# Retention's projections ahead of its heads, 15 of 16 block pairs as seven products of 384 columns

## The chip, the cores and the metric

The kernel runs on one core of a Trainium2 chip, in fp32 data. The metric is the device time of one execution in microseconds. The profile is one execution recorded by the hardware profiler; its times count from the start of the span.

## The reference, cut to the changed part

The whole program is two transformer blocks. The first layer of the second block mixes its tokens by retention: 4 heads, 512 latent and 256 context tokens (768 columns in all, the context being the last 256), width 1024, 256 query and key columns and 512 value and gate columns a head. With the additions on both sides cut away:

```python
def retention_mixer(a_ctx, a_lat, w_in, decay_param, w_out, want_ctx):
    log_gamma = -jnp.exp(decay_param.astype(jnp.float32))
    def project(a, rope):
        q, k, v, g = jnp.split(a @ w_in, [hk, 2 * hk, 2 * hk + hv], axis=-1)
        ...
        if rope is not None:
            q, k = apply_rope(q, *rope), apply_rope(k, *rope)
        k = k * RET_DK ** -0.5
        ...
    ctx_terms, g_ctx = project(a_ctx, None)
    lat_terms, g_lat = project(a_lat, axial_rope(L, RET_DK))
    o_ctx, o_lat = bidirectional_scan(ctx_terms, lat_terms)
    def readout(o, g):
        y = rms_norm_2(o).transpose(0, 2, 1, 3).reshape(B, n, hv).astype(g.dtype)
        return (jax.nn.silu(g) * y) @ w_out
```

A weight of the scan depends only on the distance of two tokens and on the head, so the kernel computes it as scores, times a table of decays (one for each head, both directions summed), times values. The result of all heads, through w_out, is added to the tokens, and a layer norm of the context and of the latent tokens follows.

## The kernel before

Every fp32 product is made of three products of parts: an operand is split into a rounded part (hi) and the rest (lo), and TensorE runs hi by hi, hi by lo, lo by hi (L2113, L2114, L2115). Weights come through a ring of three raw slots of 512 KB on SyncE's DMA queue (`t_raw`); ScalarE casts the hi part (`t_whi`, L2435), VectorE (L2810) or GpSimd (L3494) subtracts to get the lo part (`t_wlo`).

`schedule()` writes the items of the program in order, and `Plan` then lays the instructions of each engine out in one fixed order by estimated costs. So each engine runs a static queue: an instruction that waits for a semaphore holds back all that stand behind it on its engine, its DMA issues too.

Retention, in `retention()`, goes head by head. `v_rows(h)` makes the values with tokens as rows, `decays(h)` builds the head's table from a table of distances (VectorE L3315 to L3327, ScalarE L2679 to L2682, two exponentials), `queries_keys(h)` makes four blocks of 128 query and key columns (a block of 512 latent and one of 256 context columns each, so 96 matmuls for two blocks), turns them by rope and splits them, and `attend(h)` makes scores, decayed scores and values for 6 tiles of keys. `gates(h)` then makes four blocks of gate columns; between them VectorE computes the root mean square (a reciprocal at L3399), the normed values (L3405), the gated values (L3409) and their lo parts (L3414), for each block of 512 and 256 columns. Last comes the output product (`ret_o`), which reads those parts, with the next head's `v_rows` and `decays` ahead of it. In the last head there is no next head, the context's columns go first, and the layer norm of the context tokens runs on VectorE while the latent columns' products go on.

Elsewhere the kernel has a form of product that the change takes up: in the three feed-forward parts (`seven_products`), two blocks of weights by two groups of 384 tokens and two halves of the depth are multiplied with seven products in place of eight. A block matrix product with quarters A11 to A22 of the weights and B11 to B22 of the tokens is made of seven products: P1 = A11 B11, P2 = A12 B21, P3 = S4 B22, P4 = A22 T4, P5 = S1 T1, P6 = S2 T2, P7 = S3 T3, where S1 to S4 are sums of weight quarters (VectorE, `wadd`) and T1 to T4 sums of token quarters (`token_sums`, `last_sums`). P1, P6 and P7 accumulate one on another in one PSUM bank, and P5 and P3 in another, so the bank is copied out (`snap`, ScalarE) between them, and VectorE adds the copies to what comes after (`seven_add`). A product is 12 matmuls of 384 columns.

## Time and profile before

| what | value |
|---|---|
| time, median of 3 runs | 2790.18 us (2788.88 to 2790.49) |
| the profiled execution, its span | 2789.8 us |
| TensorE busy | 2760.5 us, 99% of the span |
| VectorE busy | 1891.0 us, 68% |
| ScalarE busy | 1236.5 us, 44% |
| GpSimd busy | 405.2 us, 15% |
| retention, from its first value matmul to its last output matmul | 916.25 to 1572.25 us |

The profiled execution's span lies inside the range of the three times, so what is around the span is under a microsecond. A busy share is taken over the whole span; a matmul's own time overlaps that of the one behind it, so the rate of TensorE is read from start to start, or from a stretch and its count of matmuls, and not from mean times. A slice of the page is a fortieth of the span, 69.7 us: retention covers slices 14 to 23.

### The profile page before, as it was taken

How to read it: one execution, taken by the hardware profiler on the slowest of the kernel's cores; microseconds unless marked ns; L12 is line 12 of the kernel's file. 1: busy time of each engine (PE TensorE's matmuls, PEld its weight loads, DVE VectorE, ACT ScalarE, POOL GpSimd, SP SyncE). 2: the span in 40 equal slices, each digit the busy share in tenths (PEclk: the TensorE clock that was granted, in tenths of full speed). 3: DMA queues.
4: the chain of work that ended last, by engine and by line, in shares of the span. 5: the costliest groups of instructions: out<-in, count | busy, mean ns of one | idle time of the engine just before them, and what ended most of it. 6: DMA issues, size and time to landing. Idle time of an engine off the chain costs nothing.

```text
span 2789.8 us, 42554 instructions
## 1 busy us (share of the span) xinstructions
PE 2760.5 (99%) x16554; PEld 2456.6 (88%) x16554; DVE 1891.0 (68%) x3427; ACT 1236.5 (44%) x2249; POOL 405.2 (15%) x222
## 2 busy tenths in 40 slices
PE   8999999999999999999999999999999999999998
PEld 8888896988888888888888999999997787989898
DVE  7788788868896653444435896566685636777686
ACT  5332358642233552332314654344355546545354
POOL 2233300023323011011011000000001323000000
PEclk9999999999999999999999999999999999999999
DMA  6565512236554211111011112222223121222322
GB/s 206 186 187 190 165 64 83 84 102 222 189 188 137 77 53 61 38 61 61 31 61 53 40 57 79 63 67 72 72 76 102 50 76 52 76 84 91 106 92 84
DMA packets 86025, 267.91 MB, mean 96 GB/s; under 512 B 9153, under 2 KB 18753, under 8 KB 85569
## 3 DMA queue, kind: packets, MB, share of 16 engines
q1 hardware_dynamic: 85824, 265.20, 29.6%
q8 instruction: 131, 2.15, 0.3%
q14 instruction: 70, 0.57, 0.1%
HBM read 261.49 MB, written 2.10 MB: 94 GB/s over the span
## 4 chain that ended last, share of the span: by engine, by line
PE 94%; DVE 3%; ACT 1%; issue 1%; DMA 1%; SPq 0%; DVEq 0%; ACTq 0%
PE ps L2113 30%; PE ps L2114 29%; PE ps L2115 29%; PE ps L2392 1%; PE ps L2376 1%; PE ps L2365 1%; DMA t_x<-in_x 0%; DVE t_wlo L2810 0%; PE ps L2257 0%; PE ps L2249 0%; PE ps L2308 0%; PE ps L2265 0%; PE ps L2298 0%; DVE t_m L3128 0%; DVE t_m L2927 0%
## 5 line engine op out<-in xcount | busy, mean ns | idle before, releaser
L2113 PE MATMUL ps<-t_h,t_whi 128*128 128x512 f32 (+2 forms) x2152 | 726.7, 338 | 7.7 <-DVE t_tmp L2840 3.2
L2114 PE MATMUL ps<-t_h,t_wlo 128*128 128x512 f32 (+2 forms) x2152 | 721.2, 335 | 0.0
L2115 PE MATMUL ps<-t_h,t_whi 128*128 128x512 f32 (+2 forms) x2152 | 721.1, 335 | 0.0
L2435 ACT CAST t_whi<-t_raw 128x1024 fp32r<-128x1024 f32 (+3 forms) x449 | 367.8, 828 | 570.5 <-PE ps L2115 372.6
L2113 PEld LDWEIGHTS ps<-t_h,t_whi 128*128 128x128 f32 x2152 | 407.9, 190 | 51.0 <-issue 10.4
L2114 PEld LDWEIGHTS ps<-t_h,t_wlo 128*128 128x128 f32 x2152 | 408.0, 190 | 36.5 <-issue 1.2
L2115 PEld LDWEIGHTS ps<-t_h,t_whi 128*128 128x128 f32 x2152 | 407.9, 190 | 35.6
L2113 PE MATMUL ps<-t_hid,t_whi 128*128 128x256 f32 (+2 forms) x1320 | 428.2, 324 | 1.8 <-DVE t_hid L3107 1.7
L2114 PE MATMUL ps<-t_hid,t_wlo 128*128 128x256 f32 (+2 forms) x1320 | 425.7, 322 | 0.0
L2115 PE MATMUL ps<-t_hid,t_whi 128*128 128x256 f32 (+2 forms) x1320 | 425.1, 322 | 0.0
L2810 DVE TENSOR_TENSOR t_wlo<-t_raw,t_whi 128x512 fp32r<-128x512 f32 (+3 forms) x360 | 321.7, 903 | 111.8 <-ACT t_whi L2435 108.7
L3494 POOL TENSOR_TENSOR t_wlo<-t_raw,t_whi 128x1024 fp32r<-128x1024 f32 (+1 forms) x89 | 219.4, 2465 | 902.1 <-ACT t_whi L2435 902.1
L3059 DVE CUSTOM_DVE_ANT_0 t_m<-t_raw,t_m 128x1024 f32<-128x1024 f32 x192 | 297.8, 1588 | 44.7 <-DMA t_raw<-in_ada 36.8
L2113 PEld LDWEIGHTS ps<-t_hid,t_whi 128*128 128x128 f32 x1320 | 251.1, 190 | 22.1 <-DVE t_hid L3107 2.2
L2115 PEld LDWEIGHTS ps<-t_hid,t_whi 128*128 128x128 f32 x1320 | 251.0, 190 | 18.6
L2114 PEld LDWEIGHTS ps<-t_hid,t_wlo 128*128 128x128 f32 x1320 | 251.2, 190 | 18.2
L3494 POOL TENSOR_TENSOR t_xw<-t_raw,t_xw 128x1024 fp32r<-128x1024 f32 (+1 forms) x8 | 21.4, 2670 | 724.4 <-DVE t_x L3128 517.1
L2113 PE MATMUL ps<-t_mw,t_whi 128*128 128x256 f32 (+1 forms) x394 | 121.4, 308 | 0.0
L2114 PE MATMUL ps<-t_mw,t_wlo 128*128 128x256 f32 (+1 forms) x394 | 121.3, 308 | 0.0
L2115 PE MATMUL ps<-t_mw,t_whi 128*128 128x256 f32 (+1 forms) x394 | 121.3, 308 | 0.0
L3128 DVE SCALAR_TENSOR_TENSOR t_m<-ps,t_mod,t_m 128x512 f32<-128x512 f32 (+1 forms) x79 | 51.2, 648 | 80.4 <-PE ps L2115 80.3
L2113 PE MATMUL ps<-t_wlo,t_h 128*128 128x512 f32 x264 | 104.0, 394 | 0.0
(357 smaller groups left out, 4836.5 us busy)
## 6 DMA issues: line engine op xcount, KB each, us to landing
t_raw<-in_gu SPq DMA_DIRECT2D x174, 512.0 KB, 3.4
t_raw<-in_ada SPq DMA_DIRECT2D x96, 512.0 KB, 3.8
t_raw<-in_dn SPq DMA_DIRECT2D x52, 512.0 KB, 4.2
t_raw<-in_dn SPq DMA_DIRECT2D x24, 384.0 KB, 3.4
t_raw<-in_ret_v SPq DMA_DIRECT2D x16, 512.0 KB, 3.3
t_raw<-in_ret_qk SPq DMA_DIRECT2D x16, 512.0 KB, 3.3
t_raw<-in_ret_g SPq DMA_DIRECT2D x16, 512.0 KB, 3.4
t_raw<-in_ret_o SPq DMA_DIRECT2D x16, 512.0 KB, 3.8
```

What stands on the lines that cost most here:

```text
L2113: e.matmul(out, whi, xlo, start=first, stop=False, skip_group_check=shared)
L2114: e.matmul(out, wlo, xhi, start=False, stop=False, skip_group_check=shared)
L2115: return e.matmul(out, whi, xhi, start=False, stop=last, skip_group_check=shared)
L2365: done = e.matmul(m.PS[:, hd, :].rearrange("p (a t) -> p a t", a=2), m.na_q(qpart, it.c, it.b * P, P)[pp], m.na_keys(kpart, it.c, BAND0[it ...
L2376: done = e.transpose(m.PS[:, 2 + hd, kt * P:(kt + 1) * P], s[:, kt * P:(kt + 1) * P], m.ident)
L2392: done = e.matmul(m.PS[hd * 64:hd * 64 + 64, 4 + hd, it.b * P:(it.b + 1) * P], m.at(v, 64), m.na_t(it.to[hd])[:, kt // 2, kt % 2 * P:(kt % ...
L2435: e.copy(m.block(0, it.slot, n), m.raw(it)).then_inc(*S["hi"].of(j))
L2810: e.tensor_tensor(m.block(1, it.slot, n), m.raw(it), m.block(0, it.slot, n), ALU.subtract).then_inc(*S["lo_dve"].of(j))
L3059: e.tensor_tensor_reduce(m.at(ADA_OUT + who * 1024, 1024), m.RAW[:, it.raw % NR, :], m.cond(who), 1.0, 0.0, ALU.mult, ALU.add, m.mod(it.la ...
L3128: e.scalar_tensor_tensor(out=out, in0=ps, scalar=m.mod(it.layer, it.who, it.gm, it.j), in1=old, op0=ALU.mult, op1=ALU.add).then_inc(*S["dr ...
L3494: e.tensor_tensor(m.block(1, it.slot, n), m.raw(it), m.block(0, it.slot, n), ALU.subtract).then_inc(*S["lo_pool"].of(j))
```

## The change

In the new kernel all projections of retention come first, and the heads follow.

1. The first head's values are made as before, but aside (in the tile `HID`), and stored to device memory (`s_v`, two halves of 1.5 MB).
2. The token sums T1 to T4 for 384 columns are made for retention too. The four heads' decay tables are built one behind another in one place (`RTAB`), and each is stored (`s_dec`, 768 KB); the next one may overwrite the place only when the store is done (`late`, the semaphore `d_ds`).
3. One pair of gate blocks (head 1, the first) is made in the plain way with stores to `s_g`. The other 15 pairs, in the order of heads 1, 2, 3, 0 and in each head two query/key pairs and then its gate pairs, are made by `seven_pair`, with rope on halves of 384 columns and stores to `s_qk` and `s_g`. Head 0's queries and keys stay in place.
4. Then, for each head, `attend(h)`, `v_rows(h + 1)` and `ret_o`, with the tables, the queries and keys and the gates loaded back on SyncE's queue, between the loads of weights. The gates' products no longer stand between the values and the output product. Normed and gated values are written to a place of their own (`ret_yr`).

The stores are issued on ScalarE's queue. The diff, cut to its core:

```diff
+        def decays(h, after):
+            put("ret_decay", h=h, after=after, slot=[e for k in range(4) for e in slots.get(("b", k), [])])
             free([("b", k) for k in range(4)], ("ret_gs", h))
-            ov["p"][0] = ov["p"][0] + [("ret_act", ("ll", h))]
-            ov["p"][1] = ov["p"][1] + [("ret_act", ("ll", h))]
+            put("dec_store", h=h)
+            return [("d_ds", h)]
...
+        def plain_gates(h, i):
+            def post(g, c):
+                off, after, keys_ = tmp("a", g.n)
+                half = 2 + g.t0 // 512
+                put("g_plain", h=h, c=c, half=half, g=g.id, bank=g.bank, t0=g.t0, n=g.n, off=off, after=after)
+                gate_store(h, c, half, g.t0, g.n, off, keys_, f"d_gp{off // 256}")
+            columns([(("ret_g", h * 4 + c), (SLOT,), DC, ("h", 4), [(0, "drain_act", lambda g, c=c: post(g, c))]) for c in (2 * i, 2 * i + 1)], SEG2)
...
+        def seven_pair(what, h, i):
+            key, n = ("ret", what, h, i), 384
+            ops = pair(*((("ret_qk", i * 8 + h * 2 + k) if what == "qk" else ("ret_g", h * 4 + 2 * i + k)) for k in range(2)))
+            banks = {"P1": bank(), "P2": bank(), "P5": bank()}
+            banks.update(P6=banks["P1"], P7=banks["P1"], P4=banks["P1"], P3=banks["P5"])
+            ids = {}
+
+            def product(name, q, x, before):
+                j = ops[q]
+                ready(j)
+                g = put("seven", w=j, slot=where[j], lo=low[j], name=name, f="ret", ver=4, x=x, n=n, bank=banks[name],
+                        first=name in ("P1", "P2", "P5"), before=before)
+                ids[name] = g.id
+                tick(4 * (n + 32) / 800)
+                over(j, "ps", g.id)
+
+            def snap(name):
+                off, after, keys_ = wide(n, "a")
+                put("snap", key=(*key, name), g=ids[name], bank=banks[name], n=n, off=off, after=after)
+                return off, keys_
...
+            product("P1", "A11", "B11", seat(banks["P1"], "drain_dve" if what == "qk" else "drain_act", (*key, "C21")))
+            s1, keys1 = snap("P1")
+            product("P5", "S1", "T1", seat(banks["P5"], "drain_dve", (*key, "C12")))
+            s5, keys5 = snap("P5")
+            product("P6", "S2", "T2", [("snap", (*key, "P1"))])
+            s2, keys2 = snap("P6")
+            offs, at = {(0, 0): s1, (0, 1): s2, (1, 1): s5}, (0, 1, 2, 3)
+            product("P3", "S4", "B22", [("snap", (*key, "P5"))])
+            add("C12", "P6", s2, "P3")
+            if what == "g":
+                gate("C12", 0, 1, s2, keys2)
+            product("P7", "S3", "T3", [("snap", (*key, "P6"))])
+            add("C22", "P5", s5, "P7")
+            if what == "g":
+                gate("C22", 1, 1, s5, keys5)
```

(The rest of a pair is P2 with C11 and P4 with the last quarter; for queries and keys the rope operations stand in place of the gates' silu.) The order of the whole:

```diff
+        ov["v"] = state["hid_free"]
         v_rows(0)
-        pro = state["misc_free"]
-        put("ret_setup", after=pro)
-        ov.update(oc=pro, p=[pro, pro, pro], st=pro, sg={0: pro, 512: pro})
-        decays(0)
+        put("v_store")
+        pro = state["misc_free"] + [("ps", ("root", "nf2", s)) for s in range(2)] + [("ada", (1, 47, who)) for who in range(2)]
+        put("ret_setup", after=pro + state["hid_free"])
+        token_sums("ret", 4, 384, pro)
+        last_sums("ret", 4, 384, pro)
+        late = pro
         for h in range(n_head):
-            queries_keys(h)
+            late = decays(h, late)
+        put("rope_load", after=[("ret_act", ("ll", n_head - 1))])
+        sides[:] = [late] * 4
+        plain_gates(1, 0)
+        wide_slots(384)
+        ov["qk"] = [[("d_vs0", 0)], [("d_vs0", 0)]]
+        state["quad"] = [("gate_pool", ("f2", "rs", s)) for s in range(2)]
+        for h in (1, 2, 3, 0):
+            for w in range(2):
+                seven_pair("qk", h, w)
+            for w in range(h == 1, 2):
+                last = seven_pair("g", h, w)
+        back_to_slots(384)
+        last_h = [("ps", last["P4"])]
+        rope_done = sides[0] + sides[1] + sides[2] + sides[3]
+        put("dec_load", h=0, after=rope_done + [("d_ds", n_head - 1)])
+        put("v_load", after=[("ps", last["P6"])])
+        put("g_load", h=0, after=last_h + stores[0])
+        ov.update(oc=last_h, p=[rope_done, rope_done, last_h], v=[])
...
```

On ScalarE, at the start of the projections, the old kernel has the following behind the last rows of values (`t_mw<-ps`): casts of weights, the exponentials of head 0's table, and then the scaling of the tokens by alpha (L2523).

```order
L2576 CAST t_mw<-ps 128x512 [waits ps]
L2435 CAST t_whi<-t_raw 128x1024 [waits ps,d_ring0]
L2576 CAST t_mw<-ps 128x512
L2679 ACTIVATE t_m<-t_m 128x896 [waits ret_dve]
L2681 ACTIVATE t_m<-t_m,t_tmp 128x640
L2682 ACTIVATE t_tmp<-t_m,t_tmp 128x640
L2695 CAST t_hid<-t_tmp 128x512 [waits qk]
L2523 ACTIVATE t_x<-t_x 128x256 [waits h_hi]
L2523 ACTIVATE t_x<-t_x 128x256
```

In the new kernel, behind the casts of the last token sums (L2604) come the decays' first exponential with a table load, the stores of the values, and the same scaling of the tokens (L2661, three in a row with a wait, eight times: the first rows of it here).

```order
L2604 CAST t_mw<-t_m 128x384 [waits t_full] x4
L2810 ACT_TABLE_LOAD
L2810 ACTIVATE t_tmp<-t_par 128x8
L2832 DMA s_v<-t_hid 128x3072 [waits drain_act,drain_dve]
L2832 DMA s_v<-t_hid 128x3072
L2661 ACTIVATE t_x<-t_x 128x256 [waits h_hi]
L2661 ACTIVATE t_x<-t_x 128x256 x2
```

Behind these and four casts stand the silu of the plain gate pair (L2851), its stores (L2864) and the copies of P1 and P5 out of PSUM (L2578).

```order
L2851 ACTIVATE t_tmp<-ps 128x512 [waits h_lo]
L2851 ACTIVATE t_tmp<-ps 128x256 [waits h_lo]
L2864 DMA s_g<-t_tmp 128x512 [waits drain_act]
L2864 DMA s_g<-t_tmp 128x256 [waits drain_act]
L2573 CAST t_whi<-t_raw 128x512 [waits ps,wadd]
L2573 CAST t_whi<-t_tmp 128x512 [waits ps,wadd]
L2851 ACTIVATE t_tmp<-ps 128x512 [waits d_gp0]
L2851 ACTIVATE t_tmp<-ps 128x256 [waits d_gp2]
L2864 DMA s_g<-t_tmp 128x512 [waits drain_act]
L2864 DMA s_g<-t_tmp 128x256 [waits drain_act]
L2578 COPY t_tmp<-ps 128x384 [waits d_gp0]
L2578 COPY t_tmp<-ps 128x384 [waits d_gp2]
```

So the silus (`t_tmp<-ps`), before spread under the gates of each head, now stand behind the token scaling, and of the second blocks' silus and the copies each waits for a store (`d_gp0`, `d_gp2`).

A little further on ScalarE stand the last two of the four tables, and then the copy of P6 out of PSUM.

```order
L2817 ACTIVATE t_m<-t_m 128x896 [waits d_ds,ret_dve]
L2819 ACTIVATE t_m<-t_lru,t_tmp 128x640
L2820 ACTIVATE t_tmp<-t_lru,t_tmp 128x640
L2825 DMA s_dec<-t_m 128x1536 [waits ret_gs,ret_ll]
L2817 ACTIVATE t_m<-t_m 128x896 [waits d_ds,ret_dve]
L2819 ACTIVATE t_m<-t_lru,t_tmp 128x640
L2820 ACTIVATE t_tmp<-t_lru,t_tmp 128x640
L2578 COPY t_tmp<-ps 128x384 [waits ret_gs,h_lo]
L2825 DMA s_dec<-t_m 128x1536 [waits ret_ll]
```

Before, one table was built in each head, with no store, as these rows of VectorE show:

```order
L3315 TENSOR_SCALAR t_m<-t_m,t_tmp 128x896 [waits x_sum,ret_dve,d_misc]
L3318 TENSOR_SCALAR t_tmp<-t_m,t_tmp 128x896 [waits hid_lo]
L3321 TENSOR_TENSOR t_m<-t_m,t_tmp 128x896 [waits ret_dve]
L3324 TENSOR_TENSOR t_m<-t_m,t_con 128x128 [waits ret_act]
L3327 TENSOR_TENSOR t_m<-t_m,t_tmp 128x640 [waits ret_act]
L3340 TENSOR_TENSOR t_tmp<-ps,t_m 128x512 [waits ret_gs,ps]
```

Now VectorE's row of the last table waits for the store of the one ahead (`d_ds`), and its first sum of the first pair (L3003) stands behind all four.

```order
L3491 TENSOR_TENSOR t_m<-t_m,t_tmp 128x640 [waits ret_act]
L3479 TENSOR_SCALAR t_m<-t_lru,t_tmp 128x896 [waits d_ds]
L3482 TENSOR_SCALAR t_tmp<-t_lru,t_tmp 128x896 [waits ret_gs]
L3485 TENSOR_TENSOR t_m<-t_m,t_tmp 128x896 [waits ret_dve]
L3488 TENSOR_TENSOR t_m<-t_m,t_con 128x128 [waits ret_act]
L3491 TENSOR_TENSOR t_m<-t_m,t_tmp 128x640 [waits ret_act]
L3003 TENSOR_TENSOR t_tmp<-t_tmp,ps 128x384 [waits snap,ps]
L3003 TENSOR_TENSOR t_tmp<-t_tmp,ps 128x384 [waits ps]
```

What moved: the copy of P6 (`snap`, L2578) stands behind all four tables on ScalarE, and so does the first `seven_add` on VectorE.

On SyncE's queue, around the end of the last pair, the loads for the first head stand behind the loads of the next weights:

```order
L2148 DMA t_raw<-in_ret_v 128x1024 [waits lo_dve,hi] x3
L2148 DMA t_raw<-in_ret_v 128x1024 [waits lo_pool,hi]
L2148 DMA t_raw<-in_ret_o 128x2x512 [waits lo_dve,hi]
L2148 DMA t_raw<-in_ret_o 128x2x512 [waits lo_pool,hi]
L2195 DMA t_m<-s_dec 128x1536 [waits rq_lo,d_ds,rq]
L2202 DMA t_mw<-s_v 128x1024 [waits d_vs0,ps]
L2202 DMA t_mw<-s_v 128x1024
L2205 DMA t_mw<-s_v 128x2048 x2
L2214 DMA t_m<-s_g 128x4x512 [waits d_gs2,d_gs5,d_gs1,d_gs0,d_gs3,d_gs4,ps]
L2215 DMA t_m<-s_g 128x4x256
```

Before, this head's table and gates were not loaded at all.

In the last head, VectorE had, before, reciprocal, norm, gate and lo part under the gates' products:

```order
L3399 RECIPROCAL t_tmp<-t_tmp 128x512 [waits drain_act]
L3405 TENSOR_TENSOR t_m<-t_m,t_tmp 128x512 [waits ret_dve]
L3409 TENSOR_TENSOR t_m<-t_m 128x512 [waits drain_act,ret_n]
L3405 TENSOR_TENSOR t_m<-t_m,t_tmp 128x256
L3409 TENSOR_TENSOR t_m<-t_m 128x256 [waits drain_act,ret_n]
L3405 TENSOR_TENSOR t_m<-t_m,t_tmp 128x512
L3414 TENSOR_TENSOR t_hid<-t_m,t_hid 128x512 [waits ret_act]
L3414 TENSOR_TENSOR t_hid<-t_m,t_hid 128x256 [waits ret_act]
L3409 TENSOR_TENSOR t_m<-t_m 128x512 [waits drain_act,ret_n]
L3405 TENSOR_TENSOR t_m<-t_m,t_tmp 128x256
L3414 TENSOR_TENSOR t_hid<-t_m,t_hid 128x512 [waits ret_act]
```

Now these rows come behind one another with the context's output product and layer norm between them (`t_x<-ps` is the output product's sum, L3092 and L3173 belong to the norm):

```order
L3575 RECIPROCAL t_tmp<-t_tmp 128x512 [waits drain_act]
L3293 SCALAR_TENSOR_TENSOR t_x<-ps,t_mod,t_x 128x256 [waits ps] x3
L3092 TENSOR_TENSOR t_m<-t_m,t_x 128x256 [waits drain_dve,acc] x3
L3098 TENSOR_TENSOR t_m<-t_m 128x256 [waits acc]
L3581 TENSOR_TENSOR t_m<-t_m,t_tmp 128x512 [waits ret_dve]
L3173 TENSOR_TENSOR t_x<-t_x,ps 128x256 [waits ps]
L3173 TENSOR_TENSOR t_x<-t_x,ps 128x256 x4
L3092 TENSOR_TENSOR t_m<-t_m,t_tmp 128x256 [waits sq,acc_act] x2
L3092 TENSOR_TENSOR t_m<-t_m,t_tmp 128x256 [waits sq,acc]
L3173 TENSOR_TENSOR t_x<-t_x,ps 128x256 x3
L3092 TENSOR_TENSOR t_m<-t_m,t_tmp 128x256 [waits sq,acc] x3
L3098 TENSOR_TENSOR t_m<-t_m 128x256 [waits acc]
```

and, some rows on, to the four lo parts (L3590) for which the latent output product waits:

```order
L3158 TENSOR_SCALAR t_tmp<-t_con,t_st 128x128
L3581 TENSOR_TENSOR t_m<-t_m,t_tmp 128x512
L3207 SCALAR_TENSOR_TENSOR t_x<-t_x,t_par,ps 128x256 [waits ps,x_mid]
L3207 SCALAR_TENSOR_TENSOR t_x<-t_x,t_par,ps 128x256 [waits x_mid] x7
L3213 TENSOR_TENSOR t_h<-t_tmp,t_h 128x256 [waits h_hi,h_full]
L3585 TENSOR_TENSOR t_m<-t_m 128x512 [waits ret_n]
L3581 TENSOR_TENSOR t_m<-t_m,t_tmp 128x512
L3585 TENSOR_TENSOR t_m<-t_m 128x512 [waits ret_n]
L3581 TENSOR_TENSOR t_m<-t_m,t_tmp 128x512
L3585 TENSOR_TENSOR t_m<-t_m 128x512 [waits ret_n]
L3590 TENSOR_TENSOR t_mw<-t_m,t_mw 128x512 [waits ret_act] x4
```

The gated values (L3585) and the lo parts, which stood one beside the other, are now split by the norm's rows, and no product of gates is left between the values and the output product.

## Rows read from the trace of the kernel before

**Rows 1.** The page: busy time, slices of TensorE's clock, the chain by engine.
```profile
PE 2760.5 (99%) x16554; PEld 2456.6 (88%) x16554; DVE 1891.0 (68%) x3427; ACT 1236.5 (44%) x2249; POOL 405.2 (15%) x222
...
PEclk9999999999999999999999999999999999999999
...
PE 94%; DVE 3%; ACT 1%; issue 1%; DMA 1%; SPq 0%; DVEq 0%; ACTq 0%
```

**Rows 2.** Windows: stretch, length, busy (instructions) of five engines, clock, DMA share, GB/s.
```profile
916.25:1572.25 656.00, 655.94 (x3590) 571.40 (x3589) 325.46 (x512) 245.16 (x402) 84.40 (x39) 1.00 0.17 55
...
949.90:983.17 33.27, 33.27 (x193) 29.53 (x192) 18.84 (x28) 14.81 (x30) 4.75 (x3) 1.00 0.28 100
983.17:1012.99 29.82, 29.76 (x148) 24.83 (x147) 13.71 (x21) 14.76 (x33) 1.93 (x2) 1.00 0.13 44
...
1047.19:1079.85 32.66, 32.66 (x146) 27.02 (x145) 10.25 (x15) 11.59 (x15) 2.40 (x1) 1.00 0.05 17
...
1501.49:1535.75 34.26, 34.26 (x195) 29.92 (x194) 20.30 (x25) 16.75 (x27) 6.09 (x3) 1.00 0.13 46
1535.75:1572.25 36.50, 36.50 (x301) 36.31 (x300) 33.27 (x76) 17.05 (x32) 2.41 (x1) 1.00 0.20 64
1700.00:1800.00 100.00, 100.00 (x579) 95.14 (x578) 64.65 (x108) 37.38 (x68) 0.00 (x0) 1.00 0.25 78
10.00:20.00 10.00, 8.07 (x65) 7.90 (x66) 9.40 (x22) 9.12 (x19) 0.00 (x0) 1.00 0.85 295
```

**Rows 3.** TensorE's timeline, two matmuls of 256 columns (start, length, what).
```profile
971.66 0.28 PE L2113 MATMUL ps<-t_h,t_whi 128*128 128x256 f32 x1
971.77 0.28 PE L2114 MATMUL ps<-t_h,t_wlo 128*128 128x256 f32 x1
```

**Rows 4.** Timelines of VectorE and ScalarE at head 0's decay table, first to last.
```profile
957.61 0.69 DVE L3315 TENSOR_SCALAR t_m<-t_m,t_tmp 128x896 f32<-128x896 f32 x1 [4.47 <-DMA t_m<-in_rope]
...
960.05 0.95 ACT L2679 ACTIVATE t_m<-t_m 128x896 f32<-128x896 f32 x1 [8.37 <-DVE t_m L3321]
...
961.63 0.91 ACT L2682 ACTIVATE t_tmp<-t_m,t_tmp 128x640 f32<-128x640 f32 x1
...
962.57 0.82 DVE L3327 TENSOR_TENSOR t_m<-t_m,t_tmp 128x640 f32<-128x640 f32 x1 [1.24 <-ACT t_tmp L2682]
```

**Rows 5.** Timelines: the last split of values, a table load, the scaling of tokens.
```profile
950.04 0.69 DVE L3368 TENSOR_TENSOR t_mw<-ps,t_mw 128x512 fp32r<-128x512 f32 x1 [2.95 <-ACT t_mw L2576]
...
937.79 1.28 ACT L2672 ACT_TABLE_LOAD   x1
...
968.36 1.34 ACT L2523 ACTIVATE t_x<-t_x 128x256 f32<-128x256 f32 x4
```

**Rows 6.** Groups by form, 1640 to 1900 us, VectorE twice and ScalarE (count, busy, mean ns).
```profile
L2810 DVE TENSOR_TENSOR t_wlo<-t_tmp,t_whi 128x512 fp32r<-128x512 f32 x23 | 15.8, 689 | 7.1 <-ACT t_whi L2435 7.0
...
L2840 DVE TENSOR_TENSOR t_tmp<-t_tmp,ps 128x384 f32<-128x384 f32 x11 | 6.1, 553 | 7.9 <-PE ps L2115 7.9
...
L2435 ACT CAST t_whi<-t_tmp 128x512 fp32r<-128x512 f32 x23 | 14.3, 622 | 13.8 <-DVE t_tmp L2831 9.6 <-DVE t_tmp L2826 3.5 <-PE ps L2115 0.6
```

**Rows 7.** DMA issues: count, size, median us from issue to landing.
```profile
t_raw<-in_ret_v SPq DMA_DIRECT2D x16, 512.0 KB, 3.3
...
t_raw<-in_dn SPq DMA_DIRECT2D x24, 256.0 KB, 2.6
...
out_x<-t_m SPq DMA_DIRECT2D x16, 128.0 KB, 1.7
...
t_m<-in_rope SPq DMA_DIRECT2D x1, 512.0 KB, 5.6
```

**Rows 8.** VectorE's timeline in the last head, behind the last matmul of values.
```profile
1509.34 3.35 DVE L3399 RECIPROCAL t_tmp<-t_tmp 128x512 f32<-128x512 f32 x1 [1.58 <-ACT t_tmp L2729]
...
1517.00 0.69 DVE L3405 TENSOR_TENSOR t_m<-t_m,t_tmp 128x512 f32<-128x512 f32 x1
1517.60 1.02 DVE L3414 TENSOR_TENSOR t_hid<-t_m,t_hid 128x512 fp32r<-128x512 f32 x2
```

More of the change, by code:

```diff
@@ L687, in rows, with rows_by_group @@
             pass
-    def rows_by_group(srcs, ver, after, key, dest, order=(4, 5, 0, 1, 2, 3), pairs=False, banks=(), early=0, low_dest=None):
+    def rows_by_group(srcs, ver, after, key, dest, order=(4, 5, 0, 1, 2, 3), pairs=False, banks=(), early=0, low_dest=None, aside=False):
         held = [block(s, (SLOT,)) for s in srcs]
@@ L1940, in ret_v, with v_row @@
         return self.MW[:, o:o + P]
+    def v_row(self, it, part):
+        o = (it.dst, it.low)[part]
+        return self.HID[:, o:o + 512] if it.aside else self.MW[:, o:o + 512]
     def ret_raw(self, at, n):
@@ L3348, in qk_lo @@
[L3348 to L3363 removed]
+        w.wait_ge("drain_dve", (*it.key, "C12"))
```

420 lines of the change are left out of this document (258 added, 162 removed).

## The prediction

> **What bounds the kernel now.** I read the page first: TensorE is busy for 99% of the span, its clock shows nines in all slices, and the chain that ended last is 94% TensorE [rows 1]. Then the windows of the stage that changes: over retention's 656.00 us TensorE is busy for 655.94, at a granted clock of 1.00, with VectorE busy for about half and ScalarE for 245 us [rows 2]. So two things count alone: how many microseconds of matmul columns there are, and every time at which TensorE has to wait. In this stage it waits nowhere. The sum is made against the span, 2789.8 us, which is the median of the runs, 2790.18, within 0.4 us.
>
> **What the seven products save.** A query/key stretch of four blocks is two pairs and takes 33.27 us, 16.64 a pair, for 96 matmuls. In the feed-forward stretch of 100 us, where 384-column products are mixed with 512 and others, 579 matmuls run; its products of mean 384 columns go by 100/579 = 0.173 us each [rows 2]. A seven-product pair has 84 of them: 14.5 us. The saving is 2.1 us a pair, 15 pairs: **-32 us**. Nothing else leaves TensorE; the gates, attention, values and output products keep their count. Everything below is the price, read as waits in the static queues.
>
> **Term 1, the start.** The values end at 949.90, where the queries begin [rows 2]. The plain gate pair (16.6) and P1 (12 matmuls, 2.1) bring TensorE to 968.6. P5 needs bank 4 free, so it waits for the silu of the first gate block. On ScalarE this stands behind the last T4 casts, a table load, 24 token scalings, four casts and another table load. VectorE splits the last values but one at 950.0 to 950.7 [rows 5] and then has 32 operations of 384 columns and 8 of 512 ahead of the last T4 sum. These last 0.55 and 0.69 us; one of 512 at 1517.00 is followed by the next at 1517.60, so each starts some 0.09 before the other's end, which makes them 0.47 and 0.60: 19.8 us, to 970.5 [rows 6, 8]. ScalarE adds 0.5 for the cast, 1.28, 24 times 0.335 = 8.0, four casts of 0.62 less overlap = 2.1, 1.28 and the silu 0.7 [rows 5, 6]: 984.4. TensorE waits **16 us**. Before, the same scalings lay under products that needed nothing of ScalarE.
>
> P6 then needs the copy of P1, which waits for the store of the second gate block's silu, which itself waits for the store of the first. A load of 256 KB takes 2.6 us from issue to landing, one of 512 KB 3.3 [rows 7]; two landings and a silu and two casts between give 991.8 to 993.4, against 986.5 at which P6 could start: **6 us**.
>
> P6 and P3 end at about 997. P7 accumulates on P6 and waits for the copy of P6, which is behind all four decay tables on ScalarE, and each table waits for the store of the one before. One table takes from 957.61 to the end of the sum at 962.57 + 0.82, 5.8 us [rows 4], all of it in series (VectorE, ScalarE, VectorE). The landing of a 768 KB store is in no row. The nearest from below is the 128 KB store, 1.7 us, from above the 512 KB load that took 5.6; loads of 256 and 512 KB in the ring take 2.6 and 3.3 [rows 7], 0.7 more for each 256 KB, so 4.0 for 768, and I add 0.5 because it goes to device memory from one queue with loads beside it: 4.5, with 1.7 and 5.6 as bounds. The first table's sum is done at about 998.1 (copies at 993, table load 1.28, exponentials, sum); three more periods of 4.5 + 5.8 make 1029, the copy 1029.5. The wait is **33 us** (24 to 36). Start in all: 16 + 6 + 33 = **55**, bounds 45 to 59.
>
> The Trainium skill ("DMA: Bandwidth & Descriptors", the section Anatomy of one DMA) gives about 2.0 us plus bytes by 436 GB/s for a transfer: 3.8 us for 768 KB, which would make the start 53 instead of 55. The same section warns that completion is slowest towards device memory, which these stores are and hardly any row of before shows.
>
> **Term 2, the pairs.** For a query/key pair VectorE has 13 operations of 384 columns (three sums, six of rope, four lo parts), six of 128, and eleven weight operations of 512: 13 x 0.47 + 6 x 0.2 + 11 x 0.60 = 13.9 us against 14.5 of TensorE [rows 6]; a gate pair 14 operations, 8 us. It is nearly level in two pairs of four, and the rope operations stand between sums that free banks. Nothing at the low end, 10 us at the high (8 query/key pairs by 1.3): **4 us**.
>
> **Term 3, the first attention.** SyncE reaches the table's load when the ring's slots for the next weights come free, at the end of the last pair; then come 0.77 MB of table and 3.1 MB of values. The heaviest stretch moves 295 GB/s [rows 2]: 13.3 us, plus the fixed part of a load (3.3 us less 512 KB at that rate, 1.5 [rows 7]) plus some 1.7 for the last slot. Latent values are in place 16.5 us after the last product; attention wants them after eight or nine (four score tiles, the context's values, one score tile). **8 us**; if the gates' 1.6 MB behind them on the queue share the rate it is 5.3 more, 14 in round numbers, and 3 if SyncE gets there 5 us early.
>
> **Term 4, the last head.** Before, 34.26 us of gates stood between the last value and the output product, and under them lay the reciprocal (3.35 us, from 1509.34, 7.9 us after the values' end), norm, gate and lo parts [rows 2, 8]. Now only the context's output product is there, 96 matmuls of 0.117 us, 11.3 us [rows 3]. The latent ones need lo parts that stand behind the reciprocal and behind some 42 further operations (VectorE's rows of the norm): the sum of squares comes 2 us later than now, so the reciprocal ends at 13.2; then 8 operations of 512 at 0.60, 31 of 256 at about 0.36 (by the same overlap) and three small ones, 16.5 us in all, and the norm's round trip through TensorE and ScalarE with a table load, about 2.5. The first lo part comes at 32, TensorE was ready at 11.5: **20 us** (15 to 24). In the other heads the next head's `v_rows`, 32.66 us [rows 2], cover this: nothing; without them each would cost the same 20.
>
> The reload of tables, queries and gates for heads 1 to 3 lies under those rows too: 5.5 MB a head at 295 GB/s is 19 us of 32.66. Nothing.
>
> **Sum.** 2790 - 32 + 55 + 4 + 8 + 20 = **2845 us**.
>
> **The rivals.**
> (a) *The waits stand, but the stores land fast.* For: the one store of the trace takes 1.7 us. Against: it is a sixth of the size. Start 45, terms 2 to 4 at 0, 3 and 15: 2790 - 32 + 63 = 2821. Chance 0.13.
> (b) *TensorE's clock falls in the new waits.* Nothing in this trace shows it: the clock is 1.00 throughout, and in the 656 us of retention there is no idle at all to try it [rows 2]. Four waits (16, 33, 8, 20) would each be followed by a stretch at half speed; a product of 84 / 7 = 12 matmuls costs 2.1 us more then. One or two such after each wait: +8 to +17, so 2853 to 2862. Chance 0.15. The Trainium skill ("TensorE: Matmul & The Clock Gate", Part 1: The HAM clock gate) says that an idle TensorE drops to 1.2 GHz and has to earn 2.4 GHz back; by that rule 2855 is nearer than 2845.
> (c) *VectorE becomes the bound of the query/key pairs.* For: 13.9 of 14.5 us on paper, and its work hangs on ScalarE's casts. Against: in the feed-forward stretch it runs at 65 of 100 us under the same products without a wait of TensorE [rows 2]. If each of the eight pairs is 2.5 us over, +16 more: 2861. Chance 0.09.
> (d) *The other side: faster.* The mechanism is that the queue of ScalarE is never late, so that the silu is there at 968.6 and the tables' chain is hidden under TensorE's work. The rest (terms 2 to 4 at their low ends, 18 us) leaves 14 us of the saving; so the start would have to cost under 14. The first wait alone is 16, and it rests on the sum of 40 short operations. With nothing lost at the start: 2776. Chance 0.04.
> My forecast has the remaining 0.59.
>
> **How the numbers follow.** The bounds of the four terms, 45 to 59, 0 to 10, 3 to 14, 15 to 24, would make 2821 to 2865; with the clock the upper case reaches 2872, and the lower one with an undersized start 2818. Outside are (d) and the tails of (a) and (c), under 0.2. A difference of 0.2% is 5.6 us, about what the three runs could tell; all cases but (d) lie above: faster 0.04, same 0.02, slower 0.94.
>
> **What would show it.** In the profile after, TensorE loses its nines around slices 14 and 15 of retention's start, with gaps of about 16, 6 and 33 us between 968 and 1030, the last released by ScalarE's copy behind four exponentials and four stores; a pair takes 14.5 us; a gap of about 8 in the first attention, released by the load of values; a gap of 20 between the context's and the latent columns of the last output product, released by L3590. A store of 768 KB far from 4.5 us shifts the third gap by three times the difference. Wrong would be: P7 starts without waiting for the fourth table, or the T sums end before 960, or the norm's rows do not run ahead of the lo parts.

## The result: 2963.5 us, 6.2% slower, above the range

| | median | runs |
|---|---|---|
| before | 2790.34 us | 2788.88 to 2793.93 |
| after | 2963.51 us | 2962.76 to 2964.41 |

The ratio is 1.0621, 95% interval 1.0606 to 1.0636. The direction was forecast, the size was not: 173 us lost in place of 55. The time of an execution is 1.8 us longer than its span here (2962.76 us for the profiled one, its span is 2961.0), not under a microsecond longer, as I had written ahead; no comparison below depends on it.

The page of the new kernel, in the lines that answer to [rows 1]:

```profile
PE 2780.9 (94%) x16374; PEld 2488.4 (84%) x16374; DVE 2022.0 (68%) x3722; ACT 1283.8 (43%) x2369; POOL 367.9 (12%) x207
...
PE   8999999999999399999997899999989998999998
...
PEclk9999999999999699999998999999999999999999
```

TensorE has 180 matmuls fewer and waits for 6% of the span. The hole in slice 14 is the start that the prediction speaks of. A slice is 74 us, and retention ends at 1645.7, early in slice 23: slices 22 and 23 (7 and 8) are its last head and what follows it, and 30 and 34 (8 and 8) lie far behind it. For those the prediction had no term.

The start, first by who ended TensorE's waits there (us, times, longest):

```profile
PE ps L2247 <- ACT t_tmp L2578: 36.1, 4, 28.8
PE ps L2247 <- ACT t_tmp L2851: 18.2, 1, 18.2
PE ps L2247 <- DVE t_wlo L2973: 4.7, 4, 2.3
PE ps L2247 <- DVE t_tmp L3003: 2.2, 2, 1.2
```

and the timeline of ScalarE:

```profile
975.28 7.44 ACT L2661 ACTIVATE t_x<-t_x 128x256 f32<-128x256 f32 x24
982.62 2.16 ACT L2573 CAST t_whi<-t_raw 128x512 fp32r<-128x512 f32 x4
984.80 1.28 ACT L2851 ACT_TABLE_LOAD   x1
986.10 0.87 ACT L2851 ACTIVATE t_tmp<-ps 128x512 f32<-128x512 f32 x2
...
1008.09 0.95 ACT L2817 ACTIVATE t_m<-t_m 128x896 f32<-128x896 f32 x1 [5.81 <-DVE t_m L3485]
...
1017.22 0.95 ACT L2817 ACTIVATE t_m<-t_m 128x896 f32<-128x896 f32 x1 [6.65 <-DVE t_m L3485]
...
1026.35 0.95 ACT L2817 ACTIVATE t_m<-t_m 128x896 f32<-128x896 f32 x1 [6.66 <-DVE t_m L3485]
...
1029.78 0.48 ACT L2578 COPY t_tmp<-ps 128x384 f32<-128x384 f32 x1 [0.95 <-DVE t_m L3491]
```

The reader sees the 24 token scalings ahead of the silu (wait of 18.2 us, predicted 16), and the exponentials of tables 2 to 4 in steps of 9.13 us with the copy of P6 behind them (wait of 28.8, predicted 33).

Three stretches, to be read against [rows 2]:

```profile
1030.40:1257.33 226.93, 216.36 (x1212) 212.93 (x1213) 166.09 (x319) 103.50 (x198) 2.94 (x2) 0.98 0.39 138
```

```profile
1257.33:1294.46 37.13, 30.94 (x148) 26.01 (x147) 17.41 (x32) 13.47 (x27) 2.60 (x2) 0.91 0.52 196
1585.89:1645.74 59.85, 41.43 (x304) 39.45 (x303) 46.99 (x92) 17.15 (x33) 3.71 (x2) 0.83 0.10 30
```

They are the pairs from the first P7 on (1212 matmuls, 209.7 us at 0.173), the first attention (29.8 before) and the last output product (36.5 before). So far the account is: start 80.5 us for 16.6 + 8.3 of matmuls, 55.6 lost; pairs 17.2; attention 7.3 and half a microsecond in each other head; last head 23.4; together 105, less the 32 saved, 73. Retention's last matmul starts at 1645.6 against 1572.1 before.

Compared matmul by matmul, the lag then grows to 97.6 us in the feed-forward part that follows, stays at exactly that for 440 us, and grows again in the neighbourhood mixer and the last parts, to 171.2 at the end. That is 24 + 74 us in parts that the diff does not touch. The longest waits of TensorE in the last 800 us:

```profile
PE ps L2503 <- DVE t_xw L3602: 18.2, 6, 5.7
PE ps L2247 <- DVE t_h L3213: 14.8, 7, 3.5
PE ps L2247 <- DVE t_wlo L2973: 6.9, 10, 1.2
PE ps L2391 <- DVE t_tmp L3158: 6.3, 2, 5.0
PE ps L2346 <- DVE t_x L3207: 3.5, 1, 3.5
```

All are ended by VectorE. The same last part of the program, by the view of busy time, in the new kernel

```profile
2163.00:2961.00 798.00, 735.58 (x5009) 652.04 (x5007) 491.87 (x1055) 384.94 (x776) 81.81 (x67) 0.96 0.22 71
```

and in the old one

```profile
2066.00:2789.80 723.80, 708.67 (x5004) 632.64 (x5002) 489.02 (x1055) 380.00 (x776) 83.32 (x67) 1.00 0.25 79
```

(the stretch and its length, then TensorE, its weight loads, VectorE, ScalarE, GpSimd and TensorE's granted clock). VectorE has the same 1055 instructions and 492 us of work for 489, and the part takes 74 us more. The work is the same; its order is not.

The waits are not all that TensorE loses there. Behind retention they come to 73 us, where the kernel before has 9, so they make 63 of the 98 us. The other 34 are in the matmuls themselves: for the same 8002 TensorE is busy for 1234.9 us in place of 1200.8, since many run at the lower clock right behind the waits (0.96 for 1.00 in these two rows).

### The profile page after: what moved, and what is told of

It is laid out like the page before. It is cut to its first block, busy times and chain, and to the rows that moved or that the text cites. A ratio compares the mean times of both kernels' runs of the same rounds, so it can differ in the third digit from the quotient of the medians.

```text
span 2961.0 us, 42890 instructions
## 1 busy us (share of the span) xinstructions
PE 2780.9 (94%) x16374; PEld 2488.4 (84%) x16374; DVE 2022.0 (68%) x3722; ACT 1283.8 (43%) x2369; POOL 367.9 (12%) x207
## 3 DMA queue, kind: packets, MB, share of 16 engines
q1 hardware_dynamic: 92208, 287.42, 29.8%
## 4 chain that ended last, share of the span: by engine, by line
PE 50%; DVE 6%; ACT 1%; issue 1%; DMA 0%; POOL 0%; DVEq 0%; ACTq 0%; SPq 0%; POOLq 0%
PE ps L2247 16%; PE ps L2248 15%; PE ps L2249 15%; PE ps L2530 1%; PE ps L2514 1%; DVE t_wlo L2973 1%; PE ps L2503 1%; ACT t_whi L2573 1%; DVE t_x L3207 0%; DVE t_m L3207 0%; DVE t_m L3092 0%; PE ps L2391 0%; DVE t_x L3173 0%; DVE t_h L3213 0%; DVE t_m L3032 0%
## 5 line engine op out<-in xcount | busy, mean ns | idle before, releaser
L2573 ACT CAST t_whi<-t_raw 128x512 fp32r<-128x512 f32 (+3 forms) x494 | 381.1, 784 | 671.8 <-PE ps L2249 469.6
L2247 PE MATMUL ps<-t_h,t_whi 128*128 128x256 f32 (+2 forms) x1852 | 627.4, 339 | 8.2 <-DVE t_wlo L2964 2.6
L2248 PE MATMUL ps<-t_h,t_wlo 128*128 128x256 f32 (+2 forms) x1852 | 623.2, 336 | 0.0
L2249 PE MATMUL ps<-t_h,t_whi 128*128 128x256 f32 (+2 forms) x1852 | 623.0, 336 | 0.0
L2247 PEld LDWEIGHTS ps<-t_h,t_whi 128*128 128x128 f32 x1852 | 354.1, 191 | 42.5 <-issue 9.5
L2249 PEld LDWEIGHTS ps<-t_h,t_whi 128*128 128x128 f32 x1852 | 354.0, 191 | 26.3
L2247 PE MATMUL ps<-t_mw,t_whi 128*128 128x256 f32 (+2 forms) x922 | 299.3, 325 | 71.8 <-ACT t_tmp L2578 34.3
L2247 PE MATMUL ps<-t_hid,t_whi 128*128 128x256 f32 (+2 forms) x1032 | 335.6, 325 | 0.7 <-DVE t_hid L3272 0.6
L2249 PE MATMUL ps<-t_hid,t_whi 128*128 128x256 f32 (+2 forms) x1032 | 333.2, 323 | 0.0
L2248 PE MATMUL ps<-t_mw,t_wlo 128*128 128x256 f32 (+2 forms) x922 | 296.5, 322 | 0.0
L2249 PE MATMUL ps<-t_mw,t_whi 128*128 128x256 f32 (+2 forms) x922 | 296.2, 321 | 0.0
L2247 PEld LDWEIGHTS ps<-t_mw,t_whi 128*128 128x128 f32 x922 | 177.4, 192 | 81.3 <-issue 56.8
L2247 PEld LDWEIGHTS ps<-t_hid,t_whi 128*128 128x128 f32 x1032 | 196.2, 190 | 16.9 <-issue 0.9
L2249 PEld LDWEIGHTS ps<-t_hid,t_whi 128*128 128x128 f32 x1032 | 196.1, 190 | 14.8
L2248 PEld LDWEIGHTS ps<-t_mw,t_wlo 128*128 128x128 f32 x922 | 177.7, 193 | 4.1 <-issue 0.2
L2249 PEld LDWEIGHTS ps<-t_mw,t_whi 128*128 128x128 f32 x922 | 177.3, 192 | 3.8
```

The source lines that it names most:

```text
L2247: e.matmul(out, whi, xlo, start=first, stop=False, skip_group_check=shared)
L2248: e.matmul(out, wlo, xhi, start=False, stop=False, skip_group_check=shared)
L2249: return e.matmul(out, whi, xhi, start=False, stop=last, skip_group_check=shared)
L2573: e.copy(m.block(0, it.slot, n), m.raw(it)).then_inc(*S["hi"].of(j))
```

## What orders the engines

`Plan` gives every instruction a time by which it is due, and each engine but TensorE and SyncE takes, of what is ready, what is due first. The due times come from a backward pass: TensorE's products get their times in a row, and everything that a product waits for is due so much earlier. The pass needs an order of the instructions in which each stands behind all that it depends on, and takes as dependence also that each engine's instructions follow one another as in the item list:

```python
        for some in self.ops.values():
            for a, b in zip(some, some[1:]):
                left[id(b)] = 1
        for op in every:
            left[id(op)] = left.get(id(op), 0) + op.needs
        ...
        ready = [op for op in every if not left[id(op)]]
        while ready:
            op = ready.pop()
            turn.append(op)
```

If the list has a circle, all that hangs on it never comes into `turn`, and nothing says so. The changed kernel has one. A load of query and key weights stands in the list ahead of `ret_setup`, the load of the distances, since weights are asked for early. It waits for three casts and their lo parts, which free its slot. Two of the three stand in the list behind the four decay tables (`decays` for all heads is listed ahead of the gates), and the tables wait for the distances, which stand on SyncE behind that load. So `turn` holds 7287 of 22438 instructions; in the kernel before it holds all 22129. Everything from about the first table to the end of the program starts from one common late due time. A loop then spreads the due times of each engine:

```python
            for engine in ("scalar", "vector", "gpsimd"):
                end = LATE
                for op in sorted(self.ops[engine], key=lambda op: -op.due):
                    op.due = min(op.due, end - op.takes)
                    end = op.due
```

It walks from the latest to the earliest and gives the first of several equals the latest time. So on VectorE the due times fall from 2657 us, for the first of these instructions in the list, to 1528 for the last one: of what is ready, the engines as a rule take what stands last in the list, whatever TensorE needs first.

**Theory A**: the lost due times cost most of the 173 us, wherever they fall. **Theory B** is my prediction's: the waits belong to the rearrangement (stores, tables in a row, no gates in the last head), and the rest must be its traffic and its work on VectorE.

## The experiments

**1. The changed kernel with the pass mended.** It walks along the waits and along what the planner really keeps in order:

```diff
-        for some in self.ops.values():
-            for a, b in zip(some, some[1:]):
-                left[id(b)] = 1
         for op in every:
-            left[id(op)] = left.get(id(op), 0) + op.needs
+            for x, _ in op.then:
+                left[id(x)] = left.get(id(x), 0) + 1
...
-            some = [x for x, far in op.then if far] + ([after[id(op)]] if id(op) in after else [])
-            for x in some:
+            for x, _ in op.then:
```

> The changed kernel, with one edit in the planner: its backward pass, which gives each instruction the time by which it is due, walks along what waits for what, and no longer also along the order of the item list. In the changed kernel as it stands that pass reaches 7287 of 22438 instructions, because a weight load that stands in the list ahead of the load of the distances waits for casts that stand behind the decay tables, which wait for those distances; in the kernel before it reaches all. Theory A (due times lost): everything behind retention's start was ordered without due times, so the 96 us lost behind retention's last product go, the pairs and the last head run nearly without waits, and what stays is the tables' chain of four stores, some 25 to 30 us: 2780 to 2800. Theory B (my prediction's: the waits come with the rearrangement itself, and the rest from its traffic and vector work): over 2930.

Measured: 2810.14 us (2807.55 to 2811.92), ratio to before 1.0073 (1.0058 to 1.0088). 153 of the 173 us are gone with not one operation changed. That is 10 us above my range. The waits that are left stand mostly at the start, which keeps three,

```profile
PE ps L2243 <- ACT t_tmp L2574: 30.2, 3, 26.6
```

all for copies; the silu's 18.2 us are not among them. The long one is the tables' chain, as predicted for it. Over the last 730 us the longest entry of the same view is

```profile
PE ps L2243 <- DVE t_h L3209: 2.1, 3, 0.9
```

where the changed kernel has 18.2.

**2. The kernel before, with the pass cut off at the first table.**

```diff
+        cut = next(op.item.id for op in self.ops["scalar"] if op.item.kind == "ret_decay")
+        turn = [op for op in turn if op.item.id < cut]
         turn.reverse()
```

> The kernel before, with the backward pass cut off at the first decay table's item, so that the instructions from there on get no due time, and no other edit: no store, no seven-product pair, no new order of the work. Theory A: the parts behind retention lose what they lose in the changed kernel, 24 us at the first feed-forward part and 72 in the neighbourhood mixer and the last parts, and retention some more: 2870 to 2910. Theory B: 2790, since nothing of the rearrangement is in it.

Measured: 2923.31 us (2919.68 to 2924.48), ratio 1.0481 (1.0463 to 1.0498), 13 us above the range of theory A, and with nothing of the rearrangement in it. Its waits in the last 800 us:

```profile
PE ps L2367 <- DVE t_xw L3428: 18.2, 6, 5.6
PE ps L2115 <- DVE t_h L3050: 14.4, 7, 3.5
PE ps L2115 <- DVE t_wlo L2812: 6.9, 10, 1.2
PE ps L2259 <- DVE t_tmp L2995: 6.3, 2, 5.0
PE ps L2214 <- DVE t_x L3044: 3.5, 1, 3.5
```

These are the changed kernel's five, entry by entry, at the line numbers of the old one. The planned orders say the same. From 1640 us of the kernel before to the end VectorE has 1405 blocks (the rows of an item that stay together) and ScalarE 1047; this kernel and the changed one have them in one and the same order, while against the kernel before at least 335 and 191 of them have moved. Theory B has nothing to say to that.

**3. The changed kernel with one item moved**, and the planner as it was:

```diff
+        pro = state["misc_free"] + ...
+        put("ret_setup", after=pro + state["hid_free"])
         v_rows(0)
         put("v_store")
-        pro = state["misc_free"] + ...
-        put("ret_setup", after=pro + state["hid_free"])
```

> The changed kernel with the original planner, and one item moved in the list: the load of the distances (ret_setup) stands ahead of the first head's values and no longer behind them. With it the backward pass reaches all 22438 instructions. Theory A: as the run with the mended planner, or better, because the tables can begin earlier: 2765 to 2790. Theory B: an earlier load of 0.8 MB changes at most the first waits of 51 us, so 2910 to 2963.

Measured: 2787.58 us (2784.92 to 2789.39, 10 runs), ratio 0.9988 (0.9978 to 0.9997). The circle is open, all 22438 instructions have due times, and the distances land early enough for the tables to be made under the values, so the wait of 26.6 us goes too. Against the kernel before that is 0.1% less. In the order of VectorE 5 of the 1405 blocks have moved, and from the end of retention on this kernel keeps within 2.4 us of the one before. What it still shows is where the 32 saved microseconds went:

```profile
950.00:1000.00 50.00, 44.81 (x231) 40.12 (x230) 48.53 (x89) 28.49 (x50) 0.00 (x0) 0.93 0.43 156
1700.00:1800.00 100.00, 100.00 (x579) 95.11 (x578) 64.57 (x108) 37.02 (x68) 0.00 (x0) 1.00 0.25 78
```

At the start VectorE is busy for 48.5 of 50 us (token sums, tables, weight sums), and TensorE loses 10 to 12 us in small waits; the first attention loses 8, the last head some 9. The next four take these apart.

**4. Table and values of head 0 loaded ahead of the next weights.**

```diff
+                if (h, w) == (0, 1):
+                    put("dec_load", h=0, after=rope_done + [("d_ds", n_head - 1)])
+                last = seven_pair("g", h, w, behind_p6=(h, w) == (0, 1))
...
+            if behind_p6:
+                put("v_load", after=[("ps", ids["P6"])])
```

> The version with the distances' load moved up (2787.6 us), plus: head 0's decay table is loaded back before the last gate pair and its values behind P6 of that pair, both ahead of the next weights on SyncE's queue, and no longer behind them. That version still waits 7.9 us more than it should at the start of the first attention: 6.3 for the table, 1.4 because the matmuls that follow run at half rate, and a bit for the values. If the place on the queue was the cause (theory A), these go: 2778 to 2781. If the transfers are bound by the 3.9 MB they move (theory B), at most 2 us go: 2785 to 2788.

Measured: 2786.73 us (2782.66 to 2790.03), ratio 0.9985 (0.9976 to 0.9994), within noise of experiment 3 and inside theory B's range. A miss for theory A: it was right that the table's wait of 6.1 us goes, but a new one of 4.0 stands behind it, and it is not for the values either. Waits of all engines at that place:

```profile
ACT t_whi L2575 <- DMA t_raw<-in_ret_v: 5.0, 1, 5.0
DVE t_hid L3560 <- ACT t_hid L2871: 4.6, 1, 4.6
...
PE ps L2249 <- DVE t_hid L3560: 4.0, 1, 4.0
```

Read upwards: TensorE waits for VectorE's lo part of the scores, that for ScalarE's cast, and ScalarE for a cast of the next head's value weights ahead of it, whose load I had put behind 3.1 MB. So it is the place on the queue after all, of another load; experiment 8 tests that.

**5. A second plain gate pair at the start** (`plain_gates(1, 1)`, 14 pairs by seven products).

> The same version, plus: head 1's second gate pair is made in the plain way too, at the start, so 14 pairs as seven products. It costs 2.1 us of columns. Theory A: VectorE, which is busy for 97% from 950 to 1012 us there (token sums, tables, weight sums), is what TensorE waits for, some 10 us in seven small waits; a plain pair asks little of VectorE and covers most of them: 2777 to 2782. Theory B (the waits are those for the tables' stores and stay): 2789 to 2791.

Measured: 2783.70 us (2781.76 to 2788.23), ratio 0.9977 (0.9967 to 0.9986). The point estimate lies 1.7 above the range of theory A, below that of B: from 949.9 to 1180 TensorE waits 3.4 us in place of 7.4. Of the 7.4 VectorE had ended 4.5 and ScalarE's copies 2.3; what is left is nearly all for copies. So VectorE's load was most of it. The plain pair's 2.1 us of columns are paid, and 3.9 us are left, which is little against the two intervals (they overlap).

**6. The last head's second gate pair plain, behind its values.** The silu goes straight into place; the gated values of blocks 2 and 3 wait for it:

```diff
+            if h == n_head - 1:
+                ...
+                state["h_free"] = [columns([(("ret_g", h * 4 + c), ...) for c in (2, 3)], SEG2[::-1])]
...
-        w.wait_ge("d_g", h)
+        if h == 3 and c >= 2:
+            w.wait_ge("drain_act", ("g", h, c, 2 + t0 // 512))
+        else:
+            w.wait_ge("d_g", h)
```

> The same version, plus: the last head's second gate pair is made plain and behind the last values, straight into place, so 14 pairs as seven products. It costs 2.1 us of columns and puts 16.6 us of matmuls where the last head now waits some 9 us for its lo parts. Theory A (term 4 of my prediction with its cover gone): 2779 to 2783. Theory B (those waits come from VectorE being full there with the norm, so they only move): 2788 to 2791.

Measured: 2781.26 us (2780.33 to 2782.10), ratio 0.9967 (0.9954 to 0.9980), inside theory A's range. The waits for the norm's and the lo parts' rows at that place fall from 5.9 us, in experiment 3,

```profile
PE ps L2247 <- DVE t_mw L3590: 3.9, 4, 1.7
PE ps L2490 <- DVE t_tmp L3570: 2.0, 1, 2.0
```

to one of 1.2.

**7. All three.**

> All three edits on the version with the moved load; 13 pairs as seven products. If each works and they add up: 2787.6 less 8, 8 and 7, 2763 to 2770. If they cover the same wait or move it: 2775 to 2788.

Measured: 2777.03 us (2776.29 to 2781.92), ratio 0.9956 (0.9941 to 0.9971). Inside the second case's range. But the edits neither cover one another nor move: alone they gave 0.9, 3.9 and 6.3 us, 11.1 in all, and together they give 10.6. My 8, 8 and 7 were too high for each. The attention's part had not worked alone and did not work here.

**8. The same, with the values' load one step later** (behind P3, which puts it behind the last load of value weights).

> The version with all three edits (2777.0 us), with one item moved: head 0's values are loaded back behind P3 of the last pair, and so behind the last load of value weights on SyncE's queue, not ahead of it. Theory A: that weight load came late behind the 3.1 MB, and its cast stands on ScalarE in front of the casts of the decayed scores, which is the wait of 3.5 us that took the place of the table's; it goes with its half-rate matmuls: 2772 to 2774. Theory B: the transfers themselves are late, then the wait stays or grows: 2777 to 2780.

Measured: 2770.33 us (2769.71 to 2772.27, 5 runs) against 2790.57, ratio 0.9928 (0.9916 to 0.9941): the fastest, 20 us or 0.7% ahead of the kernel before. It is 1.7 us below theory A's range: not only the wait of 3.5 us at the first attention is gone, but also the 3.2 us that the matmuls behind it had lost at the lower clock. All that TensorE waits for from 916 to 1575 us:

```profile
PE ps L2259 <- ACT t_tmp L2590: 4.0, 3, 3.1
PE ps L2358 <- DVE t_m L3111: 1.2, 1, 1.2
```

It makes 13 pairs by seven products, 27.7 us fewer columns, and gets 20 of them.

**9. The tables' stores in two parts, on experiment 1.** The first exponential waits for the first part's store alone, VectorE for none:

```diff
-        e.dma_start(dram["s_dec"][it.h], m.at(RTAB, 1536)).then_inc(*S["d_ds"].of(it.h))
+        o, n, name = ((0, 896, "d_dsl"), (896, 640, "d_dsg"))[it.part]
+        e.dma_start(dram["s_dec"][it.h][:, o:o + n], m.at(RTAB + o, n)).then_inc(*S[name].of(it.h))
```

> The changed kernel with the mended planner (2810.1 us), and each decay table stored in its two parts, so that the first exponential waits only for the store of the first part, the others for that of the second, and VectorE's rows for no store at all. The wait of 26.7 us before the first pair's P7 is, by my prediction's step 3 (tables and stores in one chain), a chain of three periods of about 9 to 10 us; with the two overlapped a period is a landing of about 3 us and 2 to 3 us of work: the wait should be 12 to 16 us and the time 2796 to 2800. If the chain is bound by something else (VectorE's queue with the token sums), the wait stays over 22 and the time over 2805.

Measured: 2804.75 us (2803.25 to 2806.23), ratio 1.0050 (1.0036 to 1.0063). The wait before P7 fell from 26.6 to 16.8 us, just above the 12 to 16 that I gave, but the time by 5.4 only, to 5 us above my range. Of the 9.7 us the wait before P6 takes back 1.7: it grew from 2.65 to 4.36. Behind it TensorE fell to the lower clock, which it had not done behind 2.65 us (0.58 granted from 973 to 980, where experiment 1 has 1.00), and matmuls below the full rate cost 2.7 us more than there. So the chain is one of landings, as predicted, and one of its links is longer than the rest:

```profile
977.56 0.83 ACTq L2830 DMA_DIRECT2D s_v<-t_hid  x2
978.43 1.20 ACTq L2823 DMA_DIRECT2D s_dec<-t_m  x1
...
987.64 0.83 ACT L2817 ACTIVATE t_m<-t_lru,t_tmp 128x640 f32<-128x640 f32 x1 [6.04 <-DMA s_dec<-t_m]
```

This store of 320 KB lands after 9.2 us, with the 3 MB of values issued just ahead of it on the same queue; the ones before and after it of that size took 2.6 and 2.2.

**10. Experiment 8 with the split stores.**

> Both together: all edits and the split stores. In the version with all edits no wait for tables is left at the start, so no change beyond 1 us against the version without the split: 2771 to 2775.

Measured: 2772.10 us (2767.97 to 2774.95), ratio 0.9928 (0.9912 to 0.9943): no difference, as expected.

## Why the prediction was wrong, point by point

The step that failed is **the sum itself**: it has a term for each stage of retention and none for the 1218 us behind it, which it put at nothing without a reason. "Nothing else leaves TensorE" is true and was taken to mean that nothing else changes. But the order of VectorE, ScalarE and GpSimd is computed for the whole program at once, and the edit took its due times away from retention to the end. The orders of the untouched parts had changed in hundreds of places; I read the new order only where the diff pointed. 98 us of the 171 lie there (24 and 74), and experiment 2 shows them without the rearrangement (28 and 72). Every sign that I had named to look for lies in retention, so most of them came and none could have told.

**The saving, -32**: right. A product of 384 columns goes by 0.173 us a matmul in the new stage as in the old one.

**Term 1, the start, 55 (45 to 59)**: 55.6. The three waits are where I put them, 18.2, 4.0 and 28.8 for 16, 6 and 33, 51.0 together, and the rest are matmuls at half rate behind them, which I had kept out. That the sum fits to 0.6 us is luck. The waits alone are 4 us under it, and the half rate fills that up. In the third wait a period of the tables took 9.13 us where I had 10.3 (a landing of 3.2, not 4.5), which makes 3.5 us less in three, but the first table was done at 1002.4 and not at 998.1, 4.3 us more. The reason, too, was half wrong. I took the place of the token scalings and of the copies in ScalarE's queue for a property of the change. With due times (experiment 1) the first wait is gone; with the distances loaded earlier (experiment 3) the last one too.

**Term 2, the pairs, 4 (0 to 10)**: 17.2, the term mis-sized most. 10.6 us of it are waits, the rest matmuls below the full rate, of which the first 1.6 belong to the wait before P7. I summed VectorE's work (13.9 of 14.5 us) and did not ask in which order it comes; without due times it comes late. With them the pairs from 1012 us to the first attention lose 1.5 us (experiment 3) to 3.4 (experiment 1).

**Term 3, the first attention, 8 (3 to 14)**: 7.3, near by luck, for the cause is another: the decay table, not the values, ends the wait (6.2 us, L3553), and 1.2 us are half-rate matmuls. What ends last was only found by taking the first away, in experiments 4 and 8.

**Term 4, the last head, 20 (15 to 24)**: 23.4. The rows that hold TensorE up are the ones that I named, the norm's rows ahead of the lo parts, but not in one gap of 20 us. They are five, 18.4 together, and only the last is ended by a lo part:

```profile
1595.10 1.12 PE L2490 MATMUL ps<-t_tmp,t_con 128*128 128x512 f32 x2 [1.49 <-DVE t_tmp L3570]
1603.01 0.70 PE L2346 MATMUL ps<-t_m,t_con 128*128 128x256 f32 x2 [2.84 <-DVE t_m L3098]
1609.08 1.22 PE L2383 MATMUL ps<-t_con,t_m 128*128 128x128 f32 x4 [5.37 <-DVE t_m L3098]
1611.44 1.23 PE L2391 MATMUL ps<-t_tmp,t_con 128*128 128x128 f32 x4 [1.14 <-DVE t_tmp L3158]
1620.24 0.58 PE L2247 MATMUL ps<-t_mw,t_whi 128*128 128x256 f32 x1 [7.58 <-DVE t_mw L3590]
```

The other 5.0 are matmuls below the full rate. With due times the loss is some 10 (5.9 of waits in experiment 3).

**Rival (b), the clock**: real; it belonged in the sum. TensorE's rows at the first attention:

```profile
1260.02 0.28 PE L2249 MATMUL ps<-t_hid 128*128 128x256 f32 x1
1266.48 0.80 PE L2247 MATMUL ps<-t_hid 128*128 128x512 f32 x1 [6.19 <-DVE t_m L3553]
1267.08 0.63 PE L2248 MATMUL ps<-t_hid 128*128 128x512 f32 x1
1267.51 0.63 PE L2249 MATMUL ps<-t_hid 128*128 128x512 f32 x1
```

Behind 6.2 us of idle the starts are 0.43 us apart, where 512 columns take 0.227: the lower of the two levels, 1.2 GHz. This trace agrees with the rule that I had cited from the Trainium skill ("TensorE: Matmul & The Clock Gate", Part 1: The HAM clock gate). Behind the wait of 28.8 us the starts of 384 columns are 0.32 us apart for 0.173 until 1033.7, and P5, behind the one of 18.2, goes wholly at that rate. A wait of the start and of the first attention cost 1.1 to 2.3 us more by it. In all, matmuls below the full rate made some 18 of the 105 us lost within retention and 34 of the 98 behind it, where short waits follow one another; (b) had 8 to 17 for its four waits.

**Rival (a)**, stores that land fast, was right as to the stores (3.2 us) and wrong as to the time. **(c)** did not happen as told: the pairs lost 17 us to VectorE's order, and with due times, at the same sum of work, 1.5 to 3.4. **(d)**, faster, did not happen, but it was nearer to what the rearrangement is worth than my sum: once the due times are there it is level (2787.6 with one item moved), and 2770.3 with three edits more. The Trainium skill's formula ("DMA: Bandwidth & Descriptors", Anatomy of one DMA) gave an estimate of 3.8 us for 768 KB; the section fits it to transfers that GpSimd issues, and these are issued by ScalarE. Measured are 3.2 us for three of the four stores and 4.8 for the last, which had the load of the rope tables in flight; the tables' loads took 5.8 to 7.9.

What stays open: experiment 2 lost 28 us within retention (one wait of 17.0 for the first head's rope rows is most of it) and 28 just behind it, the changed kernel 24 just behind it; I did not take apart which of the reordered rows cost these. Nor is it tested why the lost due times cost nothing in the long feed-forward stretch between, from 1640 to 2066 us. The orders differ least there: at least 52 of VectorE's 467 blocks have moved, where it is 81 of 156 from the end of retention to 1640, and 283 of 938 behind 2066.

## What to carry to other kernels

When one order is computed for the whole program, an edit in one stage can cost anywhere: compare the order of the parts that the diff does not touch, and if they moved, find out why before pricing a single wait. A planner that leaves out what it can't sort should stop, not go on; here one item, listed 16 places too late, cost 5% of the program (experiment 1; put ahead of the weight load, it opens the circle). And a wait seen in a static queue may be the sickness or its symptom: undo the suspected cause in the old kernel (experiment 2) as well as in the new one, and the two together settle it.

## What the runs showed of the hardware

- After the idle of 6.2 us at the first attention TensorE's next six matmuls of 512 columns start 0.43 us apart; from 1272.2 us on they start 0.23 apart. Behind the wait of 18.2 us the clock was still at the lower level when the idle of 4.0 us before 995 came, and it stayed there until 999.6. At one and the same place an idle of 2.65 us (experiment 1) left the granted clock at 1.00, and one of 4.36 (experiment 9) was followed by 0.58.
- Stores from ScalarE's queue in the changed kernel: 768 KB landed after 3.2 us, 192 KB after 2.0. Loads of 768 KB on SyncE's queue took 7.0 in the median, among others in flight. In experiment 9 a store of 320 KB landed after 9.2 us behind two of 1.5 MB on its queue, two others of its size after 2.6 and 2.2.
- A load moved ahead on a queue pays with the one that it passes. In experiment 4 that one's cast stood at the head of ScalarE's queue, and the wait of 6 us came back as one of 4.
